# The first expert phase of a hybrid decoder block laid out anew: one pair of heads per step, marks three deep, two grid stages, eight-part steps, 80 products of tile 0 in the mixer

## The reference

```python
def peer_ffn(h, w_q, sub_keys, u_tab, v_tab):       # 8 heads, 128 keys, top 16, u and v: 16384 x 1024
    q = jnp.einsum('bsd,dk->bsk', h, w_q).reshape(b, s, PEER_HEADS, 2, PEER_DKEY // 2)
    scores = jnp.einsum('bshcd,hcnd->bshcn', q, sub_keys)
    s1, i1 = lax.top_k(scores[..., 0, :], PEER_TOPK)
    s2, i2 = lax.top_k(scores[..., 1, :], PEER_TOPK)
    cand = s1[..., :, None] + s2[..., None, :]       # 16 x 16 per head
    top_s, pos = lax.top_k(cand, PEER_TOPK)
    ids = take(i1 * PEER_NKEYS + i2, pos)            # 8 x 16 experts per token
    gates = jax.nn.softmax(top_s, axis=-1)
    act = gelu(einsum('td,tkd->tk', h, u_tab[ids])) * gates
    return einsum('tk,tkd->td', act, v_tab[ids])
```

## Time and profile before

| | us |
|---|---|
| median of 3 runs | 3636.15 (3626.55 to 3640.84) |
| the profiled execution | 3633.03 |
| its span in the trace | 3631.3 |
| mean granted TensorE clock | 0.881 of 2.4 GHz |

### The profile page before, as it was taken

How to read it: one execution, slowest core, us unless ns; L and a number is a source line. 1 busy time by engine, 2 the same in 40 slices (tenths; PEclk the granted TensorE clock), 3 DMA queues, 4 the chain that set the end, 5 groups by cost and what they waited for, 6 DMA issues and landing times.

```text
span 3631.3 us, 31990 instructions
## 1 busy us (share of the span) xinstructions
PE 2954.5 (81%) x10195; PEld 1466.3 (40%) x10195; DVE 1948.0 (54%) x4610; ACT 557.6 (15%) x1043; POOL 1580.0 (44%) x1444
## 2 busy tenths in 40 slices
PE   8999988884425545556399999999999999999997
PEld 3455545542214313333144444444444444444443
DVE  2335434684799677866475656455565544441113
ACT  1321133221004402444110000000000000000000
POOL 0010001241455365576336666655567666553331
PEclk9999979887766677666699999999999999999998
DMA  3000202332875597777779999999999999997883
GB/s 111 34 24 24 83 26 87 125 109 98 320 293 187 185 408 283 269 267 275 306 278 403 409 398 417 400 360 417 380 383 409 389 417 410 409 378 277 314 311 136
DMA packets 307573, 981.52 MB, mean 270 GB/s; under 512 B 29904, under 2 KB 57680, under 8 KB 306640
## 3 DMA queue, kind: packets, MB, share of 16 engines
q0 software_dynamic: 184320, 671.17, 48.1%
q1 hardware_dynamic: 120464, 307.85, 22.2%
q10 hardware_dynamic: 2624, 0.46, 0.1%
HBM read 941.63 MB, written 37.75 MB: 270 GB/s over the span
## 4 chain that ended last, share of the span: by engine, by line
PE 34%; DMA 12%; POOL 12%; issue 7%; DVE 6%; ACT 2%; DVEq 0%; ACTq 0%; SPq 0%; POOLq 0%
PE part L1659 10%; PE hid L1640 10%; DMA v_ring<-in_peer_v_dram,ids_t 9%; POOL u_ring L1578 6%; PE acc L1687 5%; POOL v_ring L1587 5%; PE turn_ps L1631 4%; PE part L1668 3%; DVE u_ring L1947 2%; DMA gate_grid<-room 2%; POOL dense_sums L1608 1%; ACT dense_sums L1728 1%; DMA u_ring<-in_peer_u_dram,ids_u 1%; DMA keys_pair<-in_peer_keys_dram 1%; ACT dense_sums L1726 0%
## 5 line engine op out<-in xcount | busy, mean ns | idle before, releaser
L1947 DVE CUSTOM_DVE_ANT_0 u_ring<-u_ring,x_rows_in 128x1024 f32<-128x1024 f32 x608 | 743.0, 1239 | 472.4 <-DMA u_ring<-in_peer_u_dram,ids_u 456.1
L1587 POOL DMA_INDIRECT v_ring<-in_peer_v_dram,ids_t x640 | 674.4, 1054 | 605.2 <-PE acc L1687 422.5
L1578 POOL DMA_INDIRECT u_ring<-in_peer_u_dram,ids_u x608 | 676.9, 1113 | 449.6 <-DVE dots L1947 276.7
L1640 PE MATMUL hid<-x1t_dense,dense_u 128*128 128x384 f32 x2048 | 698.4, 495 | 1.2 <-issue 1.2
L1659 PE MATMUL part<-room,weights 128*128 128x512 f32 x1536 | 682.7, 594 | 9.2 <-DMA room<-in_peer_v_dram 8.9
L1640 PEld LDWEIGHTS hid<-x1t_dense,dense_u 128*128 128x128 f32 x2048 | 383.7, 192 | 338.4 <-issue 103.4
L1687 PE MATMUL acc<-v_ring,line 128*32 128x512 f32 x2560 | 348.7, 668 | 118.0 <-DMA v_ring<-in_peer_v_dram,ids_t 117.8
L1659 PEld LDWEIGHTS part<-room,weights 128*128 128x128 f32 x1536 | 291.1, 191 | 352.8 <-issue 325.1
L1668 PE MATMUL part<-dense_sums 128*128 128x128 f32 x768 | 175.4, 405 | 241.4 <-ACT dense_sums L1728 130.9
L1755 ACT ACTIVATE weights<-hid 128x384 f32<-128x384 f32 x128 | 62.8, 490 | 1463.8 <-PE hid L1640 1463.8
L1918 DVE TENSOR_TENSOR dense_sums<-dense_sums,part 128x512 f32<-128x512 f32 x186 | 126.6, 685 | 254.2 <-PE part L1659 253.8
(11 more groups left out here) (312 smaller groups left out, 2588.7 us busy)
## 6 DMA issues: line engine op xcount, KB each, us to landing
wq_pair<-in_peer_wq_dram SPq DMA_DIRECT2D x32, 2048.0 KB, 14.7
dense_u<-in_peer_ut_dram SPq DMA_DIRECT2D x128, 512.0 KB, 7.0
room<-in_peer_v_dram SPq DMA_DIRECT2D x128, 512.0 KB, 8.7
gate_grid<-room SPq DMA_DIRECT2D x6, 4096.0 KB, 15.8
room<-gate_grid SPq DMA_DIRECT2D x32, 768.0 KB, 18.0
w_ring<-in_w_in_dram SPq DMA_DIRECT2D x5, 2048.0 KB, 7.9
v_ring<-in_peer_v_dram,ids_t POOLq DMA_INDIRECT x640, 9.3
u_ring<-in_peer_u_dram,ids_u POOLq DMA_INDIRECT x608, 9.2
```

The costliest lines, as they stand in the source:

```text
L1578: pool.indirect_dma_start(u_ring[:, n % U_RING, :], None, peer_u, bass.IndirectOffsetOnAxis(ap=ids_u[:, q, k:k + 1], axis=0))\
L1587: pool.indirect_dma_start(v_ring[:, n % V_RING, :], None, peer_v, bass.IndirectOffsetOnAxis(ap=ids_t[:, q % 2, token:token + 1], axis=0))\
L1640: last = mm.matmul(hid[:, 0:DT], ud[:, c % UD_RING, k, :], x1td[:, k, :], start=(k == 0), stop=(k == KC - 1))
L1947: vec.tensor_tensor_reduce(u_ring[:, n % U_RING, :], u_ring[:, n % U_RING, :], x1[:, q % 2, :], 1.0, 0.0, ALU.mult, ALU.add, dots[:, q % 2 ...
```

## The change

The sizes are the same in sum: the same choices, gathers, chunks and groups are made. What changes is where they stand, in 151 steps instead of 176:

- The mixer makes 80 products of tile 0 instead of 32, four an item from n = 22 to n = 41.
- Pairs of tiles 1, 2, 3, 4 fall at every step, 0 to 15, and VectorE does all four parts of a pair in the step behind it (parts 1, 3, 5, 7 of now eight parts). Tile 5's pairs are at 20, 23, 26, 29; tiles 6 and 7 every six steps from 40 and 72.
- Grid groups fall eight a step, at steps 6 to 9, 10 to 13, 14 to 17. Marks are three deep (`HELD`), and two stages alternate (`stages`); to make room, `ud`, `weights` and both stages share `room`, and the dense u ring is first loaded at step 16, once the stage under it is stored. g and b of the last norm are loaded behind the grid.
- The u rows of tile 0 left over (48) fall at steps 0 to 5, eight a step; those of tile 4 at 17 to 32, eight a step; the rest four a step. Tile 0's quads are at steps 6 to 14 (2, 4, 4, 4, 4, 4, 4, 4, 2), the other tiles' from 33, 65, 97, one a step, the last tile's at 129 to 144, two a step.
- The chunks are steps 18 to 145.
- Each step is cut: eight parts on GpSimd and VectorE, four quarters on TensorE and ScalarE, so that gathers, marks, groups and quads take turns.

```diff
-FIRST_SLOTS = 2 * TOPK
+FIRST_SLOTS = 5 * TOPK
@@ products
-                return (2, 2, 3, 4)[k % DA_HEADS]
+                return 4
@@
-CHOSEN_AT = {1: 0, 4: 8, 2: 16, 3: 24, 5: 40, 6: 54, 7: 86}
-PAIR_STEPS = {1: 2, 4: 2, 2: 2, 3: 2, 5: 2, 6: 6, 7: 6}
+CHOSEN_AT = {1: 0, 2: 4, 3: 8, 4: 12, 5: 20, 6: 40, 7: 72}
+PAIR_STEPS = {1: 1, 2: 1, 3: 1, 4: 1, 5: 3, 6: 6, 7: 6}
-DENSE_AT = 43
+DENSE_AT = 18
-U_AT = (0, 17, 50, 82, 114)
-U_EACH = (6, 4, 4, 4, 4)
-V_AT = (18, 51, 84, 116, 148)
-LAST_V = (48, 81, 114, 146, 171)
+PARTS = 8
+QUARTERS = 4
+U_AT = (0, 17, 33, 65, 97)
+U_EACH = (8, 8, 4, 4, 4)
+V_COUNTS = ((2, 4, 4, 4, 4, 4, 4, 4, 2), (2,) + 30 * (1,), (2,) + 30 * (1,), (2,) + 30 * (1,), 16 * (2,))
+V_AT = (6, 33, 65, 97, 129)
+NORM_AT = (22, 64, 96, 128, 145)
-TOKEN_STEPS = 8
+TOKEN_STEPS = 4
+HELD = 3
+
+def share(items, i, n):
+    return items[i * len(items) // n:(i + 1) * len(items) // n]
+
+def choosing(step, part):
+    last, before = chosen_pair(step - 1), chosen_pair(step - 2)
+    if last is not None and step - 1 < DENSE_AT and part % 2:
+        return part // 2, *last
+    if last is not None and step - 1 >= DENSE_AT and part in (1, 4):
+        return part // 3, *last
+    if before is not None and step - 2 >= DENSE_AT and part in (1, 4):
+        return 2 + part // 3, *before
+    return None
@@ SyncE
             def load_u(c):
                 if c >= UD_RING:
                     sp.wait_ge(hid_done, c - UD_RING + 1)
+                else:
+                    sp.wait_ge(stage_stored[0], STAGES // 2 * 16)
@@
                     if i == STAGE_TOKENS // 4 - 1:
                         sp.wait_ge(group_kept, k + 1)
-                        sp.dma_start(g_dram[z]..., stage...).then_inc(stage_stored, 16)
+                        sp.dma_start(g_dram[z]..., stages[z % 2]...).then_inc(stage_stored[z % 2], 16)
@@ GpSimd
-                for i in range(max(len(rows), 4 * len(quads))):
-                    if i < len(rows):
-                        gather_u(*rows[i])
-                    if i < 4 * len(quads):
-                        gather_v(*quads[i // 4], i % 4)
-                for k in token_groups(s):
+                for i in range(PARTS):
+                    for n, q, k in share(rows, i, PARTS):
+                        gather_u(n, q, k)
+                    for m, q, at, j in share(v_rows, i, PARTS):
+                        gather_v(m, q, at, j)
+                    for k in share(token_groups(s), i, PARTS):
-                    if k >= 2:
-                        pool.wait_ge(group_built, k - 1)
+                        if k >= HELD:
+                            pool.wait_ge(group_built, k - HELD + 1)
@@ ScalarE
-                    if i == 0 and z:
-                        act.wait_ge(stage_stored, z * 16)
+                        if i == 0 and z >= 2:
+                            act.wait_ge(stage_stored[z % 2], z // 2 * 16)
```

More of the change, by code:

```diff
@@ L1296, in token_groups @@
     for d, t in enumerate(DENSE):
-        x = step - (CHOSEN_AT[t] + (PAIRS - 1) * PAIR_STEPS[t] + 5)
+        x = step - (chosen_step(t) + 2)
         if 0 <= x < TOKEN_STEPS:
-            return [d * QUADS + 4 * x + i for i in range(4)]
+            each = QUADS // TOKEN_STEPS
+            return [d * QUADS + each * x + i for i in range(each)]
     return []
@@ L1325, in quads_at, with quads_in, normed_at @@
         x = step - V_AT[q]
[L1326 to L1334, removed]
-    return []
-def v_ended(step, lag):
-    return LAST_V.index(step - lag) if step - lag in LAST_V else None
+        if 0 <= x < len(V_COUNTS[q]):
+            at = sum(V_COUNTS[q][:x])
+            return [(q * QUADS + s, q, s) for s in range(at, at + V_COUNTS[q][x])]
+    return []
+def quads_in(step, quarter):
+    quads = quads_at(step)
+    return [quad for j, quad in enumerate(quads) if QUARTERS - len(quads) + j == quarter]
+def normed_at(step, lag):
+    return NORM_AT.index(step - lag) if step - lag in NORM_AT else None
 def build_experts(nc, x1_dram, x1t_dram, g_dram, ids_first, top_first, dots_first, peer_wq, keys_t, peer_u, peer_v, peer_ut,
@@ L1620, in _ @@
             for s in range(STEPS):
-                pick = chosen_pair(s)
-                if pick is not None:
-                    n, t, pair = pick
-                    if t in DENSE:
-                        pe.wait_ge(dense_x1_in, ND * 16)
-                    else:
-                        pe.wait_ge(x1t_in, (SEL_TILES.index(t) + 1) * 16)
-                    pe.wait_ge(wq_in, (n + 1) * 32)
-                    pe.wait_ge(turn_read, turns)
-                    for c in range(KC):
-                        last = mm.matmul(turn_ps[:], weights_of(t)[:, c, :], wq[:, c, :], start=(c == 0), stop=(c == KC - 1))
-                    turns += 1
-                    last.then_inc(turn_written, 1)
@@ L1634, in _ @@
-                c = dense_chunk(s)
-                if c is not None:
-                    pe.wait_ge(ud_landed[c % UD_RING], (c // UD_RING + 1) * 16)
-                    if c:
-                        pe.wait_ge(hid_seen, c)
-                    for k in range(KC):
-                        last = mm.matmul(hid[:, 0:DT], ud[:, c % UD_RING, k, :], x1td[:, k, :], start=(k == 0), stop=(k == KC - 1))
-                    last.then_inc(hid_done, 1)
-                if pick is not None:
-                    pe.wait_ge(turn_read, turns)
-                    for i in range(4):
-                        last = mm.transpose(turn_ps[:, i * P:(i + 1) * P], q_sb[:, i * P:(i + 1) * P], ident[:])
-                    turns += 1
-                    last.then_inc(turn_written, 1)
@@ L1776, in _ @@
+                if (t := tile_chosen(s, 1)) is not None:
                     turns += 1
```

400 lines of the change are left out of this document (212 added, 188 removed).

## The result

The changed kernel takes 3676.6 us in the median of 4 runs (3672.8 to 3681.0), the kernel before 3638.5 on the same chip: a ratio of 1.011 (1.0082 to 1.0138), **slower by 1.1%**. The prediction was 3576.5 with a range up to 3650, so the sign is wrong and the time lies outside. The profiled execution has a span of 3679.0 (before: 3631.3), so the two traces differ by 48 us.

The account below looks back on a forecast made before the run. Hand-offs between engines were taken to bound the first expert phase, DMA and after 3200 TensorE the chunks. Last store at 1623 plus chunks of 1952 gave a span of 3575, 3576.5 us; range 3475 to 3650.

Parts of the forecast that it names:

- mixer's end: Mixer with 48 products more: +48 us (bounds 35 and 65), so the experts start at 944.
- steps 0 to 5: Expert steps with pairs and 48 u rows: 38 us to the scores, then 27 a step, 173 in all.
- steps 6 to 17: Grid steps to the last store: full steps 40 us (bounds 34 and 47), plus stalls; 506 in all, to 1623.
- bubble and steps 18 to 32: From the last store into the first chunks: 12 us left of a gap, then 18.3 a step, 275 for 15.
- steps 33 to 128: Chunks with eight rows a step and a pair every six for half of it: 96 x 14.12 = 1355 us.
- steps 129 to 144: Last chunks, two quads a step in a ring of two: alternately 17 and 15 us, 16.2 x 16 = 259.
- push on the last norm: Mixer's tail: products in items 34 to 38 delay the last norm by 10 us, much lying beside output matmuls.
- stall behind the store: Steps 8, 10, 12, 14: `wq` reload waits behind SyncE's stage store, TensorE empty 20 us each (bounds 16 and 26).
- rival B: Layout flows: the stall at even steps is covered, 80 us less, 3495 us; chance 0.28.
- Rival D: TensorE at 1.2 GHz through steps 18 to 32: 118 us more, 3695; decides below granted clock 0.72; chance 0.12.
- Rival C: Memory sets both ends: rows land after 10.1, not 7.9; +28 in steps 18 to 32, +29 in 129 to 144; 3633; chance 0.10.
- A: The forecast itself, the whole kernel at 3576.5 us, own bounds 3515 to 3625; chance 0.45.

Follow-up runs that it names:

- e9: The e5 kernel with 64 instead of 80 products in the mixer, eight rows in each of steps 0 to 7, quads from step 8: 3536.9 us.
- e1: The changed kernel with SyncE issuing the next pair's loads before it waits for and stores the grid stage, in steps 0 to 15: 3595.7 us.
- e2: The changed kernel with ScalarE copying the quad's line ahead of the grid copies of its quarter: 3642.6 us.
- e3: The changed kernel with the last tile's two quads of a step at quarters 0 and 3 instead of back to back: 3649.1 us.
- e5: The changed kernel with the edits of e1, e2 and e3 together: 3543.2 us.
- e7: The changed kernel without loading dense u from chunk 3 on (chunks 3 to 127 reuse what lies in the ring): 3579.9 us.
- e8: The changed kernel with marks two deep instead of three: 3673.4 us.
- e4: The kernel before with 80 products of tile 0 in the mixer, the remaining 48 in steps 0 to 7 of the experts: 3692.6 us.
- e6: The e5 kernel with 32 products in the mixer again, the 96 others in steps 0 to 7, quads from step 8: 3504.5 us.

## Why the prediction was wrong

Point by point (forecast, then measured in the profiled execution, us):

| step of the sum | forecast | measured | miss |
|---|---|---|---|
| mixer's end | 944 | 967.5 | +23 |
| steps 0 to 5 | 173 | 160 | -13 |
| steps 6 to 17 | 506 | 552 | +46 |
| bubble and steps 18 to 32 | 287 | 289 | +2 |
| steps 33 to 128 | 1355 | 1375 | +20 |
| steps 129 to 144 | 259 | 285 | +26 |
| end | 51 | 51 | 0 |

The misses add up to 104, the distance of 3575 from 3679. Every mechanism of the sum appeared. Four terms were too small by 20 to 46 and only one was clearly too large, and so a forecast gain became a loss. The steps that failed: the push on the last norm was put at 10 us and measured 24; the full grid step had no term for ScalarE's line, which cost 5 us in each of seven; the wait for v rows in the last 16 steps was taken 26 us too small in all; and steps 33 to 128, taken over unchanged from before, were 20 us longer.

**Mixer: +71, not +48.** The sixteen products in items 22 to 33 cost what was forecast: from the first product of item 22 to the end of item 33 it took 842.5 - 658.4 = 184.1 us before and 870.3 - 668.2 = 202.1 after, +18. Three batches behind the norm: 25.6 instead of 6.3, +19 for a forecast of 20. Two terms fail. From item 33 to the norm it took 71.7 instead of 47.5: +24, where I had taken 10 of push, on the ground that "much of it lies beside output matmuls". The rows above show the opposite: VectorE waits 3.7 and 3.3 us for rows in front of batches that stand ahead of the norm. e9, with nothing behind the norm, has this push too (+20). And 10 us were there before the first product ran. Six other versions with 80 products in the mixer (e1, e2, e3, e5, e7, e8) ended it between 959.7 and 966.3, so part of that 10 is variation between executions. With e4 the rest is shown: of 71 us paid, 32 came back.

**Steps 0 to 5: 21 to 22 a step after the scores, not 27.** I had added all of the choice and all eight products. At 0.81 DMA share and 125 of 160 us of VectorE, they overlapped better than forecast.

**Steps 6 to 17: right stall, wrong step.** The stall behind the store is the 20 us forecast (e1: 75 us over four). Full steps took 45, forecast 40, and e2 shows the 5 us: ScalarE copies grid groups in order and the quad's line behind them. I had named who waits behind SyncE but not who waits behind ScalarE. With both mended the full steps take 40.8 us (e5), the 40 of the sum. Seven times 5 are 35 of the 46; step 6 took 40.3 instead of 34 (copies at 1136.95 and 1177.29), and the last 5 I did not trace. That rival B (layout flows, 3495) is where e1, e2 and e6 lead is no merit of the forecast: in the kernel as it stood, the stall was real.

**Steps 18 to 32: right.** Rival D, TensorE held at 1.2 GHz there, did not occur: the granted clock was 0.82 with TensorE busy for 173 of 280 us, above the 0.72 below which it would have decided. By the Trainium skill, "TensorE: Matmul & The Clock Gate", section "HAM oscillation — how this bites in real kernels", short bursts between waits fall back to half rate each time. The 0.82 lies between the two levels: part of these steps ran at half rate and not all of them. It seems to have cost nothing, since TensorE waits for VectorE there. One sign was wrong: I had the first chunks 50 us apart for three; chunks 0 to 2 came 6 and 12 us apart, and chunk 3 came 52 us behind them.

**Steps 33 to 128: +20 against the forecast, +34 against before.** I took 14.12 from 85 chunks in a window of 1200 us; over the 96 chunks between the marks the kernel before needs 13.96. GpSimd's groups between the marks (2022 to 3362.6 and 1968.5 to 3343.4) have, before,

```profile
L1587 POOL DMA_INDIRECT v_ring<-in_peer_v_dram,ids_t x387 | 415.1, 1073 | 345.2 <-PE acc L1687 245.8 <-issue 99.4
L1578 POOL DMA_INDIRECT u_ring<-in_peer_u_dram,ids_u x347 | 384.0, 1107 | 196.3 <-DVE dots L1947 103.3 <-issue 93.0
```

and after

```profile
L1618 POOL DMA_INDIRECT v_ring<-in_peer_v_dram,ids_t x389 | 453.7, 1166 | 297.6 <-PE acc L1724 197.4 <-issue 100.2
L1609 POOL DMA_INDIRECT u_ring<-in_peer_u_dram,ids_u x382 | 402.3, 1053 | 210.5 <-DVE dots L1963 110.3 <-issue 100.2
```

37 gathers more, 35 of them of u rows. 37 x 0.524 MB at 398 GB/s are 49 us, an upper bound, since memory was not quite full before (389 GB/s in the mean). That bytes set the pace of this stage is shown by e7; that the additional rows are the 34 us is argued from the counts. Another part stays open: with no change of its work the stage took 24 us more in e4 (383 GB/s instead of 389), and e6, with the same steps as e5, 21 less (403 instead of 396). In both pairs the version with 32 products in the mixer is the faster one. What links the two was not tried.

**Steps 129 to 144: 17.8, not 16.2.** The mechanism was named (a ring of two, alternating quads), the wait for rows was undersized; e3 takes 27 us of it away. Rival C, memory at both ends, is no explanation: a row landed 6.2 us after its issue in these steps and 8.3 in steps 18 to 32, not 10.1. This was, with the mixer, the worst give-back against before: 213 us became 285, since these 16 steps now hold 32 quads instead of 22.

**The chances.** Most of my errors had one sign. Where I chose a value inside bounds (mixer 35 to 65, full step 34 to 47), I took one near the middle in each, as if they would cancel, and let the range end at 3650. The mixer's upper bound of 65 lies under the measured 71, and the full step's 47 just over the measured 45. A forecast in which a chain of in-order queues is packed tighter needs its upper end from the case that all terms sit at their upper bounds together: here 17 for the mixer, 7 x 7 = 49 for the full steps, 4 x 6 = 24 for the stalls and 29 for the last steps (rival C), which gives 3696. The 3625 given as A's upper bound left most of that out.

## What to carry to other kernels

When steps are merged, write down for *every* in-order engine what now stands in front of each load or small copy that another engine needs: two reorderings of a few lines on SyncE and ScalarE were worth 3% of the whole. Work may be moved ahead into a block only where its rows can be fetched ahead and something slower covers it; behind the block's last dependency it costs its full time plus the fetch. And what the first phase saves by leaving work over has to be paid in the next one, at the pace of that one's bound.

## What the runs showed of the hardware

**VectorE's product is blocked by a two-input GpSimd operation.** VectorE's timeline of the kernel after:

```profile
892.20 3.87 DVE L1115 CUSTOM_DVE_ANT_0 u_rows<-u_rows,x_first 128x1024 f32<-128x1024 f32 x1 [1.41 <-DMA u_rows<-in_peer_u_dram,ids_first]
...
896.00 3.35 DVE L1115 CUSTOM_DVE_ANT_0 u_rows<-u_rows,x_first 128x1024 f32<-128x1024 f32 x1
```

and GpSimd's:

```profile
892.65 2.33 POOL L856 TENSOR_TENSOR x<-x,g 128x1024 f32<-128x1024 f32 x1
895.16 3.11 POOL L858 TENSOR_TENSOR x<-x,b 128x1024 f32<-128x1024 f32 x1 [0.18 <-POOLq L857]
```

The same product takes 1.22 us alone. Here each ends 1.1 us after the GpSimd operation beside it (894.98 and 896.07; 898.27 and 899.35), as if it ran only then. Eight of the 80 products of this trace take over 2 us, and all eight run beside one of GpSimd's eight operations of this size. The kernel before has six such products among its 32, so this is a small part of the mixer's surplus, some 5 us for the pair that came on top. By the Trainium skill, "SBUF — State Buffer", section "SBUF: two separate sides", a VectorE operation with two SBUF inputs and a GpSimd operation share a port pair that is locked for a whole instruction; the ends above agree.

**SyncE itself can be held up while it issues behind large transfers.** The issue of the keys' 256 KB took 0.33 us in most steps of the kernel after. Behind a store and `wq` it took 8.59, 1.33, 10.20, 6.65 and 1.52 us; what decides between the long and the short ones is open. The first of them in SyncE's queue, where the 4 MB store and 2 MB of `wq` had just gone out:

```profile
1203.82 0.33 SPq L1551 DMA_DIRECT2D gate_grid<-room  x1
1204.19 0.43 SPq L1506 DMA_DIRECT2D wq_pair<-in_peer_wq_dram  x1
1205.59 8.59 SPq L1509 DMA_DIRECT2D keys_pair<-in_peer_keys_dram  x1
```

**A late load that costs nothing.** TensorE's chunk 3 waits long for dense u, whose ring is loaded only behind the last store:

```profile
1746.27 7.08 PE L1672 MATMUL hid<-x1t_dense,room 128*128 128x384 f32 x16 [42.23 <-DMA room<-in_peer_ut_dram]
```

It looked like the largest single wait of the kernel. In e7 it is gone, and chunk 15 comes only 4.5 us sooner after the last store (284.5 us; versions that keep the load, 284.4 to 293.2). TensorE then waits longer for VectorE's gated chunks, 82 us instead of 44 in steps 18 to 32: it had slack to make the late load up while VectorE worked through its rows.
